# Local attention units moved to other slabs of a fused decoder layer, and the order of bank reading on VectorE

## The reference

```python
proj = jnp.einsum('bsd,dc->bsc', x, w_in)
q_f, k_f, v_f, f_logit, q_s, k_s, v_s, g_f, g_s = jnp.split(proj, idx, axis=-1)
log_f = jax.nn.log_sigmoid((f_logit + b_forget).astype(jnp.float32))
o_f = forgetting_attention(...)      # 8 heads x 64, causal, bias c_i - c_j from cumsum(log_f)
o_f = jnp.einsum('bsc,cd->bsd', o_f.reshape(B, S, FOX_W), w_o_fox)
qs, ks = apply_rope(q_s, pos), apply_rope(k_s, pos)
o_s = sliding_window_sink_attention(...)   # 8 query heads, 2 key heads, window 128, sinks
o_s = jnp.einsum('bsc,cd->bsd', o_s.reshape(B, S, SWA_QW), w_o_swa)
merged = jax.nn.sigmoid(g_f) * o_f + jax.nn.sigmoid(g_s) * o_s
return jnp.einsum('bsd,de->bse', merged, w_out)
```

## Time and profile before

| what | value |
|---|---|
| median of 3 runs | 679.43 us (678.96 to 681.93) |
| time of the profiled execution | 679.46 us |
| its span in the profile | 677.7 us |
| TensorE matmul busy | 665.8 us, 98% |
| VectorE busy | 540.3 us, 80% |
| ScalarE busy | 392.2 us, 58% |
| GpSimd busy | 50.8 us, 7% |

### The profile page before, as it was taken

How to read it: one execution, slowest core, us unless ns; L and a number is a source line. 1 busy time by engine, 2 the same in 40 slices (tenths; PEclk the granted TensorE clock), 3 DMA queues, 4 the chain that set the end, 5 groups by cost and what they waited for, 6 DMA issues and landing times.

```text
span 677.7 us, 10965 instructions
## 1 busy us (share of the span) xinstructions
PE 665.8 (98%) x4034; PEld 594.8 (88%) x4034; DVE 540.3 (80%) x1021; ACT 392.2 (58%) x728; POOL 50.8 (7%) x74
## 2 busy tenths in 40 slices
PE   8999999999999999999999999999999999999995
PEld 6977888888888888888899999999999998888884
DVE  5579998767876226655989998888998889998888
ACT  5669687467766244524436555554554558767740
POOL 2102111111001011110200000000000000000000
PEclk9999999999999999999999999999999999999999
DMA  8236667876512886886021244334334327987302
GB/s 314 78 116 171 186 176 213 216 183 164 121 63 95 317 205 168 220 270 200 0 79 60 102 150 155 104 128 155 110 122 155 127 92 249 372 258 208 108 31 93
DMA packets 29560, 107.38 MB, mean 158 GB/s; under 512 B 3616, under 2 KB 3744, under 8 KB 26784
## 3 DMA queue, kind: packets, MB, share of 16 engines
q1 hardware_dynamic: 24624, 79.60, 34.1%
q0 software_dynamic: 4896, 27.28, 16.6%
HBM read 104.77 MB, written 25.17 MB: 192 GB/s over the span
## 4 chain that ended last, share of the span: by engine, by line
PE 89%; DVE 5%; ACT 2%; issue 2%; DMA 1%; POOL 0%; DVEq 0%; SPq 0%; ACTq 0%
PE ps L1643 12%; PE ps L1645 12%; PE ps L1644 12%; PE ps L1960 10%; PE ps L1962 10%; PE ps L1961 10%; PE ps L2028 5%; PE ps L2030 5%; PE ps L2029 5%; PE ps L1720 2%; PE ps L1706 2%; ACT rope L659 1%; PE ps L1681 1%; PE ps L1676 1%; DVE sl L982 1%
## 5 line engine op out<-in xcount | busy, mean ns | idle before, releaser
L982 DVE TENSOR_TENSOR sl<-raw,sh 128x1024 fp32r<-128x1024 f32 x46 | 56.3, 1225 | 43.6 <-ACT sh L643 43.5
L1960 PE MATMUL ps<-hTh,sh 128*128 128x256 f32 x320 | 90.6, 283 | 0.0
L1961 PE MATMUL ps<-hTh,sl 128*128 128x256 f32 x320 | 90.6, 283 | 0.0
L1962 PE MATMUL ps<-hTl,sh 128*128 128x256 f32 x320 | 90.6, 283 | 0.0
L1643 PE MATMUL ps<-xh,sh 128*128 128x512 f32 x208 | 83.6, 402 | 1.1 <-DVE q_f L1049 1.1
L1645 PE MATMUL ps<-xl,sh 128*128 128x512 f32 x208 | 81.3, 391 | 0.0
L1644 PE MATMUL ps<-xh,sl 128*128 128x512 f32 x208 | 81.1, 390 | 0.0
L643 ACT ACTIVATE sh<-raw 128x1024 fp32r<-128x1024 f32 x46 | 48.9, 1064 | 35.6 <-PE ps L1645 22.5
L1960 PE MATMUL ps<-vt,sh 128*128 128x256 f32 x240 | 68.1, 284 | 0.2 <-ACT sg L883 0.2
L1962 PE MATMUL ps<-vt,sh 128*128 128x256 f32 x240 | 67.9, 283 | 0.0
L1961 PE MATMUL ps<-vt,sl 128*128 128x256 f32 x240 | 67.9, 283 | 0.0
(11 more groups left out here) (255 smaller groups left out, 1747.6 us busy)
## 6 DMA issues: line engine op xcount, KB each, us to landing
raw<-in_slabs SPq DMA_DIRECT2D x46, 512.0 KB, 4.3
raw_f_even<-in_gu SPq DMA_DIRECT2D x10, 1280.0 KB, 5.4
raw_f_odd<-in_gu SPq DMA_DIRECT2D x10, 1280.0 KB, 5.4
item_raw<-tw SPq DMA_DIRECT2D x44, 256.0 KB, 3.1
item_raw<-in_wdn SPq DMA_DIRECT2D x33, 256.0 KB, 5.6
tw<-in_wdn POOLq DMA_DIRECT2D x11, 512.0 KB, 5.6
tw<-tw POOLq DMA_DIRECT2D x22, 256.0 KB, 4.4
x_raw<-in_xT SPq DMA_DIRECT2D x8, 256.0 KB, 5.8
```

What stands on the lines that cost most here:

```text
L982: dve.tensor_tensor(slot(sl, n, w), raw_of(n), slot(sh, n, w).bitcast(F32), ALU.subtract).then_inc(lo_ready, 1)
L1960: pe.matmul(dst, sh[:, w], bh[:, c, :], start=start and c == 0, stop=False, skip_group_check=True)
L1961: pe.matmul(dst, sl[:, w], bh[:, c, :], start=False, stop=False, skip_group_check=True)
L1962: last = pe.matmul(dst, sh[:, w], bl[:, c, :], start=False, stop=c == KC // 2 - 1, skip_group_check=True)
```

## The change

`LOCAL_STEP` and `FOX_STEP` replace the formula of `unit_step`; `WITHIN`, the banks and the waits follow. VectorE reads the slab's bank ahead of the maxima in the slabs of `WITHIN`. The zero fill of the augmented operands is split in two, and three buffers are placed elsewhere.

```diff
+LOCAL_STEP = (6, 8, 9, 11, 12, 18, 19, 20)
+FOX_STEP = 23
+UNITS_AHEAD = 5
...
-    return 6 + a if a < 8 else 19 + a - 8
...
-WITHIN = tuple(range(unit_step(2), unit_step(7) + 1)) + (unit_step(7) + 2,)
+    return LOCAL_STEP[a] if a < 8 else FOX_STEP + a - 8
...
+WITHIN = (8, 9, 10, 11, 12, 13, 18, 19, 20, 21, 22)
...
+LAST_FOX = unit_step(UNITS - 1)
...
-    return {27: 2, 28: 3, 30: 1, 32: 1}.get(n, 0)
+    return {LAST_FOX + 1: 2, LAST_FOX + 2: 3}.get(n, 0)
...
-        kl_s = at("kl_s", 104, [P, 2, SEQ], F32R)
+        kl_s = at("kl_s", 132, [P, 2, SEQ], F32R)
...
-        rope1 = [at("rope1_even", 58, [P, SEQ]), at("rope1_odd", 134, [P, SEQ])]
+        rope1 = [at("rope1_even", 58, [P, SEQ]), at("rope1_odd", 52, [P, SEQ])]
...
-            pool.wait_ge(lo_ready, 2)
             pool.memset(kl_s[:, :, :].bitcast(F32), 0.0).then_inc(key_zeros, 1)
...
                 dve.wait_ge(stackT_done, 1)
-                dve.wait_ge(pv_done, 8)
-                for t in (q_aug, k_aug):
-                    for g in range(2):
-                        dve.memset(t[zero_rows(g), g, :].bitcast(F32), 0.0).then_inc(zeros_made, 1)
+                for g in range(2):
+                    dve.memset(k_aug[zero_rows(g), g, :].bitcast(F32), 0.0).then_inc(zeros_made, 1)
...
+                if h == 0:
+
+                    dve.wait_ge(pv_done, 8)
+                    for g in range(2):
+                        dve.memset(q_aug[zero_rows(g), g, :].bitcast(F32), 0.0).then_inc(zeros_made, 1)
...
             for n in range(1, N_WOUT + KC - WOUT_TAIL + 1):
+
+                if n in WITHIN:
+                    take(n - 1)
                 for a in units_at(n, 0):
                     maxima(a)
...
-                take(n - 1)
+                if n not in WITHIN:
+                    take(n - 1)
...
-                elif a == 8:
-                    pe.wait_ge(v_taken, TB)
-                    pe.wait_ge(qk_taken, 8)
                 else:
                     pe.wait_ge(exp_done, a)
+                if a == UNITS_AHEAD:
+                    pe.wait_ge(v_taken, TB)
+                elif a == 8:
+                    pe.wait_ge(qk_taken, 8)
...
                 elif n == N_V:
-                    pe.wait_ge(exp_done, 8)
+                    pe.wait_ge(exp_done, UNITS_AHEAD)
                     pe.wait_ge(qk_taken, 7)
...
-                elif N_G < n < 27:
+                elif N_G < n <= LAST_FOX:
                     pe.wait_ge(gate_taken, n - N_G)
-                elif n in (27, 28):
+                elif LAST_FOX < n < LAST_FOX + 3:
                     pe.wait_ge(exp_done, UNITS)
-                elif n == 30:
-                    pe.wait_ge(o_sum_done, UNITS)
-                elif 28 < n < N_WO:
-                    pe.wait_ge(gate_taken, n - N_G - 1)
+                elif LAST_FOX + 3 <= n < N_WO:
+                    pe.wait_ge(gate_taken, n - N_G - 2)
                 elif n in (N_WO, N_WO + 1):
                     pe.wait_ge(exp_done, UNITS)
                     pe.wait_ge(probT_taken, UNITS)
+                    pe.wait_ge(gate_taken, N_WO - N_G - 1)
```

## The result

The changed kernel takes 698.49 us (median of 6 runs, 696.43 to 704.49) against 679.22 before. The ratio is 1.0283, with a 95% interval from 1.0263 to 1.0302: slower by 19.3 us, where 12.1 were forecast and 695.5 was the upper end of the range.

The account below looks back on a forecast made before the run. The prediction took TensorE to bound the kernel: new waits of 14.4 us less the 2.3 us that go gave +12.1, so 679.46 became 691.6 us. The range was 686.0 to 695.5 us.

Parts of the forecast that it names:

- What bounds the kernel, and the most that can be won: Attention stretch: TensorE bounds the kernel; its four waits, 2.3 us in all, are the most the change can win.
- Term 1: Transposes of unit 0, after slab 7's sixth matmul: TensorE waits for ScalarE's fourth rotation, +1.9 us (bounds 1.0 to 1.9).
- Term 2: Scores of unit 2, inside slab 9: wait for unit 1's exponentials, +2.0 us (bounds 0 to 2.7), and 0.1 at slab 8.
- Term 3: Values of unit 4, ahead of slab 14: wait for the low parts of the probabilities, +1.2 us (bounds 0 to 2.5).
- Term 4: Scores of unit 5, inside slab 18: wait until VectorE has taken four banks, +2.1 us (bounds 1.9 to 2.3).
- Term 5: Gate slabs 18 to 30 share bank 0; slabs 19 to 23 wait for ScalarE's copies, +7.1 us (3.6 to 8.0).
- Sum of waits: All new TensorE waits of the attention stretch together: 14.4 us, before taking off the 2.3 us of old waits.
- Rival A: Gate slabs: ScalarE is in time, only bare bank hand-overs and two other waits cost, +5.3, 684.8 us; chance with mixtures 0.13.
- From step 23 on: Gate slabs after the moved units: the old pattern from step 19 returns and TensorE has no gap there.
- edits at nothing: Zero fills, moved buffers, last values and weight transfers: no further cost; copies of about 3 us stay covered by 10.9 us.
- Rival C: Short TensorE waits lower the clock: 697.1 us with one slab at half pace, 718.9 with five; chance with unseen waits 0.11.

## Why the prediction had the waits right and the time wrong

- *What bounds the kernel, and the most that can be won (2.3 us).* Nothing here contradicts it. Even the version made for it won nothing that can be measured.
- *Term 1, transposes 0: 1.9.* 2.0, for the rotation and at the place that was worked out.
- *Term 2, scores 2: 2.0.* 2.2, and by the chain as written: VectorE stood idle for ScalarE's copy of slab 7 and began the maxima at 62.78, where 63.1 was worked out. With the reading behind the maxima the wait is gone. The 0.1 at slab 8 was nothing.
- *Term 3, values 4: 1.2.* 1.3. *Term 4, scores 5: 2.1.* 2.05.
- *Term 5, one bank: 7.1.* 7.3 (1.3, 1.9, 2.4, 0.9, 0.7). Its least price, 0.9 a hand-over, is the 0.93 of the later forgetting units alone; with a second bank it is gone.
- *Sum of waits: 14.4.* 14.9. The kernel with the two other causes taken away runs at 692.7; the forecast was 691.6. Rival A (684.8) is out. Of the 6.9 us between 691.6 and 698.5, the waits make only 0.5; the rest comes from the two steps that follow.
- *"From step 23 on the pattern is that of step 19 before, and TensorE has no gap there now."* **This step failed.** It is true up to the projections and was carried on to the end without a look at GpSimd, whose queue waits for the last unit. The section on edits at nothing counted ScalarE's and VectorE's work behind the last values (3 us of 10.9) and left out the third engine with 94 us of work (216.55 to 310.92) behind the same values. The chain had 13.9 us to spare, the units move by 21.8 against what follows. In the changed kernel the columns are 2.7 to 2.9 later for it. The price goes with how long the sums last: 0.35 in the profile where they took 88.1 us, 8.8 (211.0 from slab 23 to the columns, with the clock at half pace behind the wait) where they took 97.4.
- *Rival C, the clock.* **This step failed as well**, and cost more: 3.2 us in the profile. The sum has no term for the clock. It was taken as an alternative to the sum, at 0.11 with unseen waits; it comes on top of the sum. Of the waits that the prediction itself had worked out, three were 2 us or longer, and the rows of before held none longer than 1.1: "as far as they reach" was the place to widen the range. Its unit price was 5.5, a whole slab at half pace; it is about 1.6. That C's figure for one such slab (697.1) lies near the 698.5 measured is luck: two falls and GpSimd's queue together happen to be about as long.

The rule of the Trainium skill (TensorE: Matmul & The Clock Gate, section "A second HAM failure mode: psum-queue depth-cycling") says that frequent short idle times between groups of matmuls make the gate swing and cost throughput. The traces after agree in the swing and its cost, with 0.50 behind waits of 2.02 and 2.28 us in the changed kernel, though these were single waits some 90 us apart and not frequent ones; the measured figure, 1.6 a fall, decides its size.

In numbers, for the profiled executions: waits +12.6, clock +3.2, GpSimd's queue +2.9, spread thin +0.4: 19.1 of 19.0. Shown by experiments are the first three. (The opening, 0.4 shorter here, and the 0.3 of slower matmuls behind waits are not in this list; they nearly cancel.) Not settled: the last 0.4, which stand behind the start of the columns and in no profile of the experiments, and how long GpSimd's sums take. From residual load to the end of the same four sums they lasted 88.1 to 97.4 us in eight profiles. Where they end late, TensorE waits: 0.7 and 0.8 us with 91.3, 2.8 with 93.4, 6.8 with 97.4. No run here shows why they vary.

## What to carry to other kernels

When a unit of work moves, list every engine that waits for its last result, and for each the work queued behind that wait, down to the ones that are idle 93% of the time: its slack against the next meeting point, not its load, decides. A reading order or a bank that is free "earlier" wins nothing by itself; ask what it is put ahead of (here a chain maxima, exponentials, scores of the next unit) and whether anything still stands between two users of one bank. And when a sum of waits comes out, look at its longest terms again: a wait of about 2 us may be paid twice, by itself and by a halved clock behind it, so filling or splitting it is worth more than its length.

## What the runs showed of the hardware

- The granted clock fell from 2.4 to 1.2 GHz after single idle stretches of TensorE of 1.9 to 6.8 us (2.02 to 2.07 ahead of scores 2, 2.28 ahead of slab 21, 2.12, 2.83 and 6.78 ahead of the turned blocks of the layer norm), in a kernel that keeps it 96 to 98% busy otherwise. In the changed kernel each fall cost about 1.6 us. In the attention stretch it never fell behind waits of 0.3 to 1.74; but in the opening of the kernel with the later forgetting units it fell behind one of 1.07 (with one of 0.76 two us ahead of it), where the kernel before waited 1.05 and kept it.
- It does not fall behind each of them: transposes 0 waited 1.8 to 1.9 in five profiles and it stayed at 1.00; scores 5 waited 1.9 in five, and it fell in three of them and not in two; slab 21 waited 2.3 in three, and it fell in two of them.
- Small multiplications that nobody reads, shorter than the wait, kept it up in each of the waits where they stood, at no cost to be seen.
- The executions of a kernel scatter most where GpSimd's sums are late for the layer norm: 8.1 us in the changed kernel, 5.7, 6.8, 9.6, 4.3 and 9.0 in the five experiments that leave or make them late. Where they are in time it is 1.4 (with three falls of the clock in the profile), 2.3, 0.9 and 0.9, and 3.7 in 11 executions of the version with one unit behind the values. So the clock alone does not make the scatter.
